# A two-block transformer forward pass: the first drive products between the modulation chunks, a GpSimd helper, a reordered gate

## The reference

```python
cond = jax.nn.silu(c)
mod = cond @ w_ada[i] + b_ada[i]                 # 2048 -> 6 x 2048
shift1, scale1, gate1, shift2, scale2, gate2 = jnp.split(mod, 6, axis=-1)
h = _modulate(_rms(x, norm1_w[i]), shift1, scale1)        # y * (1 + scale) + shift
proj = h @ w_in[i]                               # 2048 -> 4096
u, q, k, v = jnp.split(proj, splits, axis=-1)    # u: the drive of the state space model
y_ssm = _s5_mixer(u, ...)                        # 64 groups, 64 complex states, 16 channels
y_att = _dilated_attention(q, k, v, ...)
mixed = jnp.concatenate([y_ssm, y_att], axis=-1) @ w_out[i]
x = x + gate1 * mixed
h2 = _modulate(_rms(x, norm2_w[i]), shift2, scale2)
ffn = (jax.nn.silu(h2 @ w_ffn_gate[i]) * (h2 @ w_ffn_up[i])) @ w_ffn_down[i]
x = x + gate2 * ffn
```

## Time and profile before

| what | us |
|---|---|
| median of 3 runs (lowest to highest) | 3244.72 (3244.39 to 3249.36) |
| the profiled execution | 3248.48 |
| its span in the trace | 3246.7 |
| PE busy | 3171.5 |
| DVE busy | 1814.1 |
| ACT busy | 1243.8 |
| POOL busy | 157.0 |
| last strip of `ada1` ends | 112.2 |
| first product of `w_in` starts | 124.93 |
| first `states_in` starts | 175.43 |
| last `w_lo` of the first program block | 397.17 to 399.46 |

### The profile page before, as it was taken

How to read it: one execution, slowest core, us unless ns; L and a number is a source line. 1 busy time by engine, 2 the same in 40 slices (tenths; PEclk the granted TensorE clock), 3 DMA queues, 4 the chain that set the end, 5 groups by cost and what they waited for, 6 DMA issues and landing times.

```text
span 3246.7 us, 56012 instructions
## 1 busy us (share of the span) xinstructions
PE 3171.5 (98%) x24596; PEld 3034.1 (93%) x24596; DVE 1814.1 (56%) x1689; ACT 1243.8 (38%) x1192; POOL 157.0 (5%) x182
## 2 busy tenths in 40 slices
PE   6799999999999999999999999999999999999999
PEld 3599979999999999999999999999999998998997
DVE  0699876776454545654444544555556544454454
ACT  2376634433333333433333333343334333333333
POOL 1434100000000000000000000000030000000000
PEclk7799999999999999999999999999999999999999
DMA  9876667776555555555555555566535555555554
GB/s 342 287 257 235 236 234 240 242 250 209 190 174 186 188 182 177 186 169 176 173 170 179 175 175 173 177 185 143 130 130 182 182 182 182 190 185 185 190 181 156
DMA packets 329090, 631.92 MB, mean 195 GB/s; under 512 B 22452, under 2 KB 24264, under 8 KB 328664
## 3 DMA queue, kind: packets, MB, share of 16 engines
q1 hardware_dynamic: 317896, 626.16, 59.4%
q10 hardware_dynamic: 11040, 3.51, 0.5%
HBM read 627.53 MB, written 2.10 MB: 194 GB/s over the span
## 4 chain that ended last, share of the span: by engine, by line
PE 81%; DVE 4%; issue 2%; ACT 1%; DMA 0%; DVEq 0%; ACTq 0%
PE ps L579 20%; PE ps L580 20%; PE ps L581 20%; PE ps L609 3%; PE ps L611 3%; PE ps L610 3%; PE ps L2037 2%; PE ps L2039 2%; PE ps L2038 2%; DVE w_lo L446 1%; ACT w_hi L441 1%; PE ps L2074 1%; PE ps L2076 1%; PE ps L2075 1%; PE ps L1811 1%
## 5 line engine op out<-in xcount | busy, mean ns | idle before, releaser
L446 DVE TENSOR_TENSOR w_lo<-raw,w_hi 128x2048 fp32r<-128x2048 f32 x496 | 1141.1, 2301 | 1218.1 <-ACT w_hi L441 1217.8
L441 ACT ACTIVATE w_hi<-raw 128x2048 fp32r<-128x2048 f32 x496 | 949.6, 1915 | 1676.2 <-PE ps L581 1291.3
L579 PE MATMUL ps<-act_hi,w_hi 128*128 128x258 f32 (+2 forms) x3328 | 953.9, 287 | 24.6 <-DVE w_lo L446 15.5
L580 PE MATMUL ps<-act_lo,w_hi 128*128 128x258 f32 (+2 forms) x3328 | 952.5, 286 | 0.0
L581 PE MATMUL ps<-act_hi,w_lo 128*128 128x258 f32 (+2 forms) x3328 | 950.5, 286 | 0.0
L579 PE MATMUL ps<-hid_hi,w_hi 128*128 128x256 f32 (+1 forms) x2816 | 796.0, 283 | 0.5 <-DVE w_lo L446 0.5
L580 PE MATMUL ps<-hid_lo,w_hi 128*128 128x256 f32 (+1 forms) x2816 | 795.5, 282 | 0.0
L581 PE MATMUL ps<-hid_hi,w_lo 128*128 128x256 f32 (+1 forms) x2816 | 794.3, 282 | 0.0
L579 PEld LDWEIGHTS ps<-act_hi,w_hi 128*128 128x128 f32 x3328 | 631.8, 190 | 29.1 <-issue 15.0
L580 PEld LDWEIGHTS ps<-act_lo,w_hi 128*128 128x128 f32 x3328 | 631.7, 190 | 0.1
L581 PEld LDWEIGHTS ps<-act_hi,w_lo 128*128 128x128 f32 x3328 | 631.3, 190 | 0.0
(11 more groups left out here) (371 smaller groups left out, 2810.1 us busy)
## 6 DMA issues: line engine op xcount, KB each, us to landing
raw<-in_w_ada SPq DMA_DIRECT2D x96, 1024.0 KB, 6.0
raw<-in_ffn_w_gate SPq DMA_DIRECT2D x88, 1024.0 KB, 5.2
raw<-in_ffn_w_up SPq DMA_DIRECT2D x88, 1024.0 KB, 5.1
raw<-in_ffn_w_down SPq DMA_DIRECT2D x88, 1024.0 KB, 5.1
raw<-in_w_in SPq DMA_DIRECT2D x64, 1024.0 KB, 6.6
raw<-in_w_ffn_gate SPq DMA_DIRECT2D x44, 1024.0 KB, 5.1
raw<-in_w_ffn_up SPq DMA_DIRECT2D x44, 1024.0 KB, 5.2
raw<-in_w_ffn_down SPq DMA_DIRECT2D x44, 1024.0 KB, 5.1
```

The source lines that it names most:

```text
L441: act.activation(w_hi[b][:, :, :], raw[j % RING][:, :, :], ACT.Copy).then_inc(hi_ready, 1)
L446: dve.tensor_tensor(w_lo[b][:, :, :], raw[j % RING][:, :, :], w_hi[b][:, :, :].bitcast(F32), ALU.subtract).then_inc(lo_ready, 1)
L579: pe.matmul(o, whi, hi_, start=(k == 0 and not (shared and m % 2)), stop=False)
L580: pe.matmul(o, whi, lo_, start=False, stop=False)
```

## The change

The front is taken quarter by quarter. Phase `ada1` now has 40 chunks: for each quarter of the features four V chunks of scale1 and four of shift1, then the two S chunks of the drive whose rows are this quarter. DVE sums and normalises a quarter at a time, ACT and DVE split its two chunks, and PE makes the two products (`first_in`) between the strips of the next quarter. The drive's outputs stay in PSUM over the four quarters, and ACT writes them out (`drive_out`) at the first two S chunks of `w_in`. `c_nat` is read later, and its transposes go through PE in four batches.

Phase `w_in` has the other 24 S chunks and the same 32 V chunks, in the order SVSVSVV. The 27 turns are spread over 24 S chunks by the table `SLOT_AT`, with two turns at three of them. `c_powers` moves from DVE to POOL, behind the phases of the next block. The heads' and gate1's places move accordingly.

In `ffn1.up0` the order of the chunks changes from SSVSSVSSVSSV to SSSSVSVSSVSV.

The diff, cut:

```diff
-            add(f"{name}.up{i}", groups, 2, 4, "SSVSSVSSVSSV" if name == "ffn1" and i == 0 else None)
+            add(f"{name}.up{i}", groups, 2, 4, "SSSSVSVSSVSV" if name == "ffn1" and i == 0 else None)
...
-    add("ada1", 8, 0, 4, "VVVV")
-    add("w_in", 4, 2, 4, "SV" * 8)
+    add("ada1", 1, 2, 4, "VVVVVVVVSS" * 4)
+    add("w_in", 1, 6, 4, "SVSVSVV" * 8)
...
-        BASE = 5
+        SLOT_AT = (8, 9, 10, 11, 12, 13, 14, 15, 16, 17, 18, 19, 19, 20, 21, 22, 23, 24, 24, 25, 26, 27, 28, 29, 29, 30, 31)
...
+        def drive_out(act, g):
+
+            act.wait_ge(chunk_done, 7 + g)
+            src = half_tiles(g)
+            for t in range(4):
+                for j in range(STEP):
+                    ins = act.activation(proj[32 * j:32 * j + 32, 4 * g:4 * g + 4, step_cols(t)],
+                                         src[32 * t:32 * t + 32, :, j:SEQ:STEP], ACT.Copy)
+            ins.then_inc(bank_free[g], 2)
...
                 pool.tensor_tensor(fr[:, :, :], fr[:, :, :], kk[:, :, :], ALU.subtract).then_inc(fr_ready, 1)
+                if i:
+                    c_powers(pool, i - 1)
+            c_powers(pool, BLOCKS - 1)
...
+                for q in range(QUADS):
+                    if q:
+                        strip_copy(2 * q)
+                    strip_copy(2 * q + 1)
+                    dve.wait_ge(mod_sum, 2 * q + 2)
...
+                    norm_dve(dve, q, lambda: split_lo(dve, ada, 0, 10 * q + 8))
+                    split_lo(dve, ada, 0, 10 * q + 9)
...
+                for q in range(1, QUADS):
+                    first_in(2 * q - 2)
+                    strips(2 * q, (0, 1))
+                    first_in(2 * q - 1)
+                    strips(2 * q, (2, 3))
+                    if q == 1:
                         params_pe(pe)
+                    else:
+                        c_turns(2 * q - 4)
+                    strips(2 * q + 1, (0,))
+                    group_sum(2 * q)
+                    if q > 1:
+                        c_turns(2 * q - 3)
+                    strips(2 * q + 1, (1, 2, 3))
+                    group_sum(2 * q + 1)
+                first_in(6)
+                first_in(7)
```

More of the change, by code:

```diff
@@ L1301, in states_out @@
             dve.tensor_tensor(hh[:, 1, :, :], t1[:, 1, :, :], t2[:, 1, :, :], ALU.add).then_inc(h_ready, 1)
[L1303 to L1322, removed]
-        def ssm_dve(dve, m):
[L1325 to L1331, removed]
+        def ssm_dve(dve, m):
+            for i, slot in ssm_turns(m - 1):
+                if slot == 0 and i:
+                    states_out(dve, i - 1)
+                if slot == 1 and i < BLOCKS:
+                    states_in(dve, i)
         def small_sums(pe, m, i):
@@ L1407, in sums_act @@
         def sums_act(act, m):
-            if m == 29:
+            if m == 30:
                 act.wait_ge(hs_mm, 4)
@@ L1500, in _ @@
-                act.wait_ge(c_turned, 1)
-                for r in range(2):
-                    for h in range(2):
[L1503 to L1508, removed]
-                                  beside=lambda m: (sums_act(act, m), ssm_act(act, m), heads_act(act, m)))
+                root_act(act, "norm1")
@@ L1510, in _, with beside @@
+                act.wait_ge(pool_zero, 2)
+                act.wait_ge(pre_pool, PRE_STEPS)
+                e_slots(act, 0)
+                def beside(m):
+                    sums_act(act, m)
+                    ssm_act(act, m)
+                    heads_act(act, m)
+                    if m in (8, 9):
+                        drive_out(act, m - 8)
+                flush = run_phase(act, "w_in", split_hi, bind(act, copy_out), None, beside=lambda m: beside(m + 8))
                 ssm_act(act, 32)
@@ L1606, in _, with c_turns @@
-                pe.wait_ge(acc_copied, 8)
-                gather(pe, acc1[:, 7, :], 5, 28)
-                products(pe, "w_in", act_hi, act_lo, SEQ_COLS, counted(act_ready, ACT0["norm1"]), beside=lambda m: ssm_pe(pe, m))
+                def c_turns(b):
+                    r, half = divmod(b, 2)
+                    if b == 0:
+                        pe.wait_ge(pre_act, 8)
+                    for i in range(4):
+                        mm = pe.transpose(ps[:, 6 + b % 2, P * i:P * i + P], cd[:, 8 * r + 4 * half + i, :, :].rearrange("p d n -> p (d n)"), ident)
+                    mm.then_inc(c_turned, 1)
@@ new lines, in _, with strips @@
+                ada = byname["ada1"]
+                def strips(g, js):
+                    q, part = divmod(g, 2)
+                    for j in js:
+                        if j == 0 and g >= 2:
+                            pe.wait_ge(acc_copied, g - 1)
+                        if j == 0 and g >= 5:
+                            pe.wait_ge(*((c_read, g - 4) if g < 8 else (c_ready, 1)))
+                        n = 10 * q + 4 * part + j
+                        landed(pe, ada, 0, n)
+                        for t in range(CK):
+                            pe.matmul(ps[32 * t:32 * t + 32, 7 - g % 2, :], cond32[:, CK * j + t, :], raw[n % RING][:, t, :],
+                                      start=(j == 0), stop=(j == 3)).then_inc(acc_step, 1)
@@ L1609, in _ @@
+                first_in(6)
+                first_in(7)
+                pe.wait_ge(c_ready, 1)
+                products(pe, "w_in", act_hi, act_lo, SEQ_COLS, counted(act_ready, ACT0["norm1"]), beside=lambda m: ssm_pe(pe, m + 8))
                 pe.wait_ge(y_ready, BLOCKS)
```

239 lines of the change are left out of this document (135 added, 104 removed).

## The result

The changed kernel took 3262.97 us (median of 5 runs, 3260.19 to 3265.15) where the kernel before took 3244.51 in the same session: a ratio of 1.0056, with an interval of 1.0044 to 1.0069. It is slower by 18.5 us, against a forecast of 10. Its profiled execution has a span of 3263.4 us, 16.7 more than before.

What follows compares the result with a forecast made beforehand. PE was busy nearly throughout, with transfers bounding the first 112 us and DVE's sum w_in. +23 for the first block and -13 for ffn1.up0 give +10: 3244.7 + 10 = 3255; range 3226 to 3274, the forecast's own 3247 to 3264.

Steps and rivals of the forecast that it cites:

- s0: Front: the moment when the first quarter's act_lo is done, forecast at 50 us.
- 34.3 a quarter: Front: each further quarter is a closed chain through the ring of four, s + 34.3, where ten chunks' transfers are 27.2.
- The gate's order: ffn1.up0: the new order removes three stalls of PE and the slow starts after them, -8 to -14, taken as -13.
- +23: First block, up to the end of w_in: 380 + 11 + 18 + 4 + 10 = 423, against 399.5 before.
- the tail: End of w_in: the same tail as before, 389.5 to 399.5, counted as 10.
- (1): Start of w_in: splits wait for the last products and queue with the drive copies on ACT; PE loses 11.
- (2): w_in: in four places two V chunks follow states_in and PE runs dry, 6.0 each, one maybe covered: +18.
- (3): w_in: c_powers on POOL, 10 us a block, slows DVE beside it by some 10, of which PE feels +4.
- A to D: Rivals: faster (0.25), no change (0.20), POOL becomes the bound, the reorder does nothing (last two together 0.13).
- A: Rival, w_in: second w_lo buffer covers the double V, PE keeps its clock; 3222 to 3239; chance 0.25.
- C: Rival, w_in: POOL becomes the bound, 16 beyond the forecast, 3271; 0.13 together with the rival that the reorder does nothing.
- The upper bound of +38: w_in: the loss with all four double-V places stopping PE and a POOL that falls behind.

Runs made afterwards that it cites:

- the order's best form: Changed kernel with later small sums, spread V chunks and strips of six chunks taken early: 3238.11 us with c_powers on GpSimd, 3234.46 on DVE.
- both edits of the strips: On the later-sums kernel, the first four chunks' strips ahead of products: 3243.15 us; with V chunks spread, the fifth and sixth too: 3238.11.

## Why the prediction was right, and where its sizes were off

**The front: right, step by step.** s0 was forecast at 50, and PE's first product came at 49.2; 34.3 a quarter, and it was 34.2 to 35.2; the drive's last product at 166, and it ended at 166.9. The chain (products of one quarter, strips, two transfers, sum, norm, w_lo, act_lo) was summed from durations of the kernel before, and that was enough for the time. What it left out is how soon the next wait stands behind this one: with the slots freed sooner the quarter was still 32 to 33 us, as PE then waited for transfers.

**The gate's order: right.** -13 was forecast; -13.1 stands between the two traces, and -13.0 was measured alone.

**w_in: right in sign, 5 short in size, and for a cause that the prediction had only half.** +23 was forecast for the first block, and it is 27.7. That the sum came so near is in part luck: one term was far too large and others too small. PE's time from the drive's last product to the block's end:

```profile
166.90:427.20 260.30, 230.25 (x1856) 227.83 (x1854) 225.88 (x238) 149.61 (x329) 143.02 (x137) 0.91 0.68 227
```

Of these 260 us the prediction had 214 as PE's work, 10 as the tail and 33 as (1), (2) and (3). Less work and tail, 36 are left. Term by term:

*The start, (1).* 11 were forecast on PE, and PE stood for 1.8. The waits that were meant are there, but on DVE: 14.1 us of idle time before its first three `w_lo`. No run takes this start apart, so what it is worth at the end stays open.

*The sum on DVE.* The prediction let DVE's 27 us of c_powers go, reckoned 10 for the slowing beside GpSimd, and had PE feel 4 of them in (3). That term was mis-sized too: taking c_powers off GpSimd made DVE's busy time 23.5 shorter (229.4 to 205.8), so the slowing cost what the move saved. Three pairs of windows show it, c_powers on GpSimd against c_powers on DVE: the changed kernel (229.4, 229.7), the order's best form (229.0, 229.4), and the kernel before with the gate's order (210.0, 209.1). What remained is that 7 V chunks, 22 us, which before ran beside the drive, now come after it (25 V before behind the drive's last `w_lo`, 32 now). 22 + 23.5 - 27 is 18.5, near the 20 by which DVE's work grew; so the head start of 20 was, on DVE, the same work put off, not work saved.

*GpSimd's own price.* 10 us a block were taken, and it is 10.0 (the six groups of c_powers in the trace sum to 79.8 over eight blocks). POOL still waited for PE (59.3 us before `eb`); it did not become the bound. The sign that POOL would be busy for over 20 of 27 us was not met: it was busy for 154 of 272, or 15 of 27. A block takes 34 us now, and beside c_powers POOL had 9.3 us of work in it (154 less 79.8, over eight), where the prediction had taken 12.45 from one window. Seven of the 64 operations took over 2 us, as the earlier trace rows had shown for another:

```profile
310.19 1.09 POOL L1162 TENSOR_TENSOR pm<-ctr,par 128x256 f32<-128x256 f32 x1
311.25 2.70 POOL L1163 TENSOR_TENSOR pm<-ctr,par 128x256 f32<-128x256 f32 x1
313.90 1.09 POOL L1164 TENSOR_TENSOR pm<-ctr,par 128x256 f32<-128x256 f32 x1
```

Each of the seven ran beside a `w_lo`, which took 2.72 to 2.82 then and 2.28 to 2.29 where GpSimd stood still. A V operation took 0.75 where GpSimd stood still (46 of 120), and 1.02 in the median where it worked throughout (63 of 120): slowed, but not held. The Trainium skill's rule ("SBUF — State Buffer", "Who interferes with whom") has the two engines stop each other for whole instructions; for `w_lo` the trace agrees in that it held the seven, for V it does not. The Trainium skill's advice in "Perfetto Trace Analysis", "Optimizing Scalar/DVE Operations", that moving work between DVE and GpSimd might not help, is what the three pairs show.

*PE's stops, (2).* The prediction had three at 6.0 with the slow stretch behind each, all behind two V chunks. There were five, 25.8 us of idle time together, two of them there. The other three come from a part of the change that stands ahead of the prediction and got no price in it: two turns at one S chunk put PE's small sums behind ACT's copy of y of the same chunk, 4.7 to 4.8 each. Moving the sums by one slot took 16 us away, the largest single effect in `w_in`; spreading the V chunks took some 4 more. The cause of the 16 is shown, by the edit and by the waits that went with it. What the five stops and the slower work around them cost together, some 34 of the 36 us above, stands where 22 had been forecast for (2) and (3).

*The rivals.* None of A to D came about. For A, DVE's sum would have had to fall. C had the right engine and the wrong victim: not POOL got late, but DVE. The upper bound of +38 is +40 by its own terms (11 + 24 + 15 + 10 on 380); nothing hangs on it.

Open: why the transfers still come late in each quarter after both edits of the strips, and what the start of `w_in` costs. The two stops of 4.8 that spreading left were down to 2.5 at most with c_powers on DVE, which points at the V slowed beside GpSimd; no run separates this.

## What to carry to other kernels

Work that is moved ahead of a stage helps only by what the stage's bounding engine doesn't get back: count that engine's work from the new start to the end, what is put off included. When a table packs turns tighter, look at what the first instruction of the second turn waits for; here a small sum behind a copy cost 16 us, and spreading the doubled V chunks gave back 4. And work moved between DVE and GpSimd is to be counted on both: here what stayed became slower by about what left.

## What the runs showed of the hardware

DVE beside a busier GpSimd: the 128x512 scalar_tensor_tensor took 0.90 us in the mean where it took 0.80 without c_powers, and the 128x2048 difference 2.49 where it took 2.29, although GpSimd's own instructions are small (1.1 us). I had expected less than half of it. Operation by operation it is 0.75 alone and 1.02 in the median beside a working GpSimd, and 2.29 alone against 2.62 to 2.82 (ten of eleven). A stop of PE of 4.8 us was followed by a stretch at a granted clock of 0.50, as from 341.0 to 349.2 us, in which PE was busy throughout.
